# Two on-chip buffers that begin 32 bytes later in every partition

## The reference, cut to what matters

```python
x = x + lru_mlstm_layer(rmsnorm(x, e_norm[j]), ...)    # u = x @ w_in, ..., y @ w_out
x = x + ssd_layer(rmsnorm(x, o_norm[j]), ...)          # u = x @ w_in, ..., y @ w_out
hn = rmsnorm_2(h, norm_mix_w[l]);  proj = hn @ w_in[l]
h = h + merged.astype(h.dtype) @ w_out[l]
h = h + conv_gated_mlp(rmsnorm_2(h, norm_ffn_w[l]), ...)   # u = h @ w_up, ..., @ w_down
```

## The kernel before, in words

| buffer | first byte | remainder |
|---|---|---|
| RAW, WL | 16,512 | 0 |
| WH | 45,184 | 0 |
| XN | 65,664 | 0 |
| YS1, YS2, XMS, GOS, MS, HS | 114,720 | 32 |
| XCS, DOS, ZS | 131,104, 147,488, 176,160 | 32 |
| GE1, ST, KTM, YB | 143,392, 151,072, 146,464, 197,152 | 32 |
| HB | 216,768 | 0 |

## Time and profile before

### The profile page before, as it was taken

The page is one execution under the profiler, slowest core; times in us unless marked ns, Lnnn a source line. Parts: engine busy times, 40 slices in busy tenths (PEclk is TensorE's granted clock), DMA queues, the critical chain, the costliest instruction groups (busy, mean ns, idle before and its releaser), DMA issues.

```text
span 3152.4 us, 53605 instructions
## 1 busy us (share of the span) xinstructions
PE 3073.7 (98%) x21726; PEld 2844.2 (90%) x21726; DVE 2307.0 (73%) x3156; ACT 1841.7 (58%) x2374; POOL 540.2 (17%) x640
## 2 busy tenths in 40 slices
PE   7999999999999999999999999999999999999997
PEld 7989998889999999889888889999998888888886
DVE  7655888657788887676866887876666888887544
ACT  5554888645766776555664554445445666666443
POOL 1000000000000000145634555750001000000000
PEclk9999999999999999999999999999999999999999
DMA  5445445556555556665433445556555555555554
GB/s 209 155 149 178 156 156 180 178 189 212 185 185 182 180 182 208 196 202 195 154 124 124 148 140 170 173 173 210 185 187 187 189 192 188 192 188 191 190 188 139
DMA packets 158761, 560.50 MB, mean 178 GB/s; under 512 B 17760, under 2 KB 26016, under 8 KB 158000
## 3 DMA queue, kind: packets, MB, share of 16 engines
q1 hardware_dynamic: 158512, 557.06, 53.7%
HBM read 550.64 MB, written 6.36 MB: 177 GB/s over the span
## 4 chain that ended last, share of the span: by engine, by line
PE 85%; DVE 7%; ACT 5%; issue 2%; DMA 0%; POOL 0%; DVEq 0%; ACTq 0%; POOLq 0%; SPq 0%
PE ps L574 84%; DVE WL L1355 2%; ACT WH L921 2%; ACT L911 2%; DVE XC L1329 0%; DMA RAW<-in_w 0%; DVE XMC L1329 0%; DVE XC L1345 0%; ACT RS L911 0%; DVE IB L1318 0%; POOL RSB L1957 0%; DVE X L1329 0%; DVE HB L1318 0%; PE ps L750 0%; DVE BS L1318 0%
## 5 line engine op out<-in xcount | busy, mean ns | idle before, releaser
L574 PE MATMUL ps<-XN,WH 128*128 128x256 f32 (+1 forms) x8864 | 1855.4, 303 | 17.8 <-DVE WL L1355 11.7
L921 ACT ACTIVATE WH<-RAW 128x1024 fp32r<-128x1024 f32 x1010 | 1064.8, 1058 | 1110.2 <-PE ps L574 1058.8
L1355 DVE TENSOR_TENSOR WL<-RAW,WH 128x1024 fp32r<-128x1024 f32 x1010 | 1260.4, 1255 | 478.7 <-ACT WH L921 470.8
L574 PEld LDWEIGHTS ps<-XN,WH 128*128 128x128 f32 x8864 | 1435.4, 192 | 94.0 <-DVE WL L1355 12.7
L574 PE MATMUL ps<-XN,WL 128*128 128x256 f32 x5120 | 1445.4, 282 | 0.0
L574 PEld LDWEIGHTS ps<-XN,WL 128*128 128x128 f32 x5120 | 981.7, 192 | 0.0
L574 PE MATMUL ps<-YS,WH 128*128 128x512 f32 (+1 forms) x1088 | 371.4, 388 | 7.2 <-DVE YS L1318 3.8
L574 PE MATMUL ps<-YS,WL 128*128 128x256 f32 x1056 | 296.6, 281 | 0.0
L1957 POOL TENSOR_TENSOR RSB<-RSB,SQ 128x256 f32<-128x256 f32 x75 | 75.9, 1012 | 1220.8 <-ACT SQ L911 1218.6
L574 PEld LDWEIGHTS ps<-YS,WH 128*128 128x128 f32 x1088 | 203.6, 189 | 51.9 <-DVE WL L1355 4.2
L574 PE MATMUL ps<-HS,WH 128*128 128x512 f32 x688 | 238.6, 392 | 0.0
(11 more groups left out here) (332 smaller groups left out, 3325.2 us busy)
## 6 DMA issues: line engine op xcount, KB each, us to landing
RAW<-in_w SPq DMA_DIRECT2D x1010, 512.0 KB, 3.3
CSB<-sums SPq DMA_DIRECT2D x64, 128.0 KB, 3.8
X<-scratch SPq DMA_DIRECT2D x2, 2048.0 KB, 8.0
X<-in_x SPq DMA_DIRECT2D x1, 2048.0 KB, 8.0
scratch<-X SPq DMA_DIRECT2D x1, 2048.0 KB, 8.6
scratch<-X SPq DMA_DIRECT2D x4, 512.0 KB, 5.5
out<-X SPq DMA_DIRECT2D x4, 512.0 KB, 2.7
X<-in_x SPq DMA_DIRECT2D x3, 512.0 KB, 9.0
```

Source lines behind the costliest of these rows:

```text
L574: return pe.e.matmul(dst, l, r, start=start, stop=stop, skip_group_check=True)
L921: act.e.activation(WH[:, w % NH, :], RAW[:, w % NB, :], ACT.Copy).then_inc(*act.one(("wh", w)))
L1355: dve.e.tensor_tensor(WL[:, w % NB, :], RAW[:, w % NB, :], WH[:, w % NH, :].bitcast(F32), SUB).then_inc(*dve.one(("wl", w)))
```

## The change

Two lines are added to the placement. WH begins 32 bytes later, XN with it; a second step behind XN moves all that follows by 64 bytes.

```diff
         RAW = v3(fx("RAW", NB * UB * 128), NB)
         WL = v3(Map(nc, base, end)("WL", NB * UB * 128, F32R), NB)
+        fx.at += 32
         WH = v3(fx("WH", NH * UB * 128, F32R), NH)
         XN = v3(fx("XN", 16 * 512, F32R), 16)
+        fx.at += 32
         CV = fx("CV", NVEC)
```

## The result

The changed kernel took 3159.41 us in the median of 19 runs, the kernel before 3152.9 us in 19 runs beside it: a ratio of 1.0018 (95% interval 1.0012 to 1.0025), some 6 us slower. One of the changed kernel's 19 runs, in a slow state, took 4298.83 us and is left out of the ratio. The forecast was 3124 us. The time lies inside the stated range, but on the other side of the kernel before.

What follows compares the result with a forecast made beforehand. PE was taken to bound the kernel, its time the sum of its steps. XN's -27 us, all else nothing, gave 3152.4 - 27 = 3125.4 us of span, so 3124 us of time; whole range 3117 to 3168 us.

Steps and rivals of the forecast that it cites:

- What bounds the kernel: PE, busy 98% of the span; only its step lengths matter, and the weight pipeline waits for it.
- XN at 32: Form "f" over XN, 3,744 blocks from 0.360 to 0.352 us: 30.0 us, less a tenth, so -27 us.
- WH at 32 in form "w": One of two weight loads in form "w" comes from the moved WH; steps have slack, so nothing taken.
- The other inputs: ZS, XMS, DOS, GOS, XCS, YS in form "f", 736 blocks at remainder 32: cost 0 to 5.9 us, nothing taken.
- The rest: Form "t", 384 long matmuls, would be 1 us; a tenth off XN's gain for small matmuls and waits between blocks.
- Phase: Rival, 0.27: both places set form "f"'s pace; 3145 us, or 3157 if one slow step holds its two neighbours.
- Its other case: Under phase, over XN only WL's step of three gains, 9.7 us; the other inputs lose 3.8 us: 3145 us.
- Weights off the multiple of 64: Rival, 0.19: in form "f" each WH step costs 2.6 ns over the slow pace; +17 us, 3168 us.
- No effect: Rival, 0.08: form "f"'s pace follows something else differing between XN and ZS, such as higher address bits; 3151 us.
- the 16-byte lines: Rule against the forecast: 32 bytes are two whole SBUF lines, operands cover as many as before, time stays 3151 us.

Runs made afterwards that it cites:

- the second execution: The changed kernel profiled once more with nothing altered, to see whether its paces repeat; 3162.62 us, one run.
- the faster kernels above: Against the kernel before: XN by 32, others by 128, 0.9938; XN by 192, others by 256, 0.9918; XN by 192, MLP's inputs by 288, 0.9892.

## Why the prediction was wrong

**What bounds the kernel: right.** WL's 1257 ns and WH's 1060 ns stayed, and the waits for WL are 15.9 us instead of 15.1; what moved the time were PE's steps.

**XN at 32: the size near, the reason wrong.** The forecast took 27 us off form "f" over XN, and 27.0 us went; that they agree so closely is luck. The pace fell to 117.8 ns and not to ZS's 117.3, which gave 22.5 us, and the other 4.5 are less time at the lower clock, which the second execution didn't have. Above all, the step said that the streamed operand's own place sets the pace. XN at remainder 0 over WH at 0 and WL at 32 runs at 117.8 ns (RAW and WL moved), and XN at 0 over rings at 32 at 116.9 ns (all rings moved): it is the distance to the rings that counts. By the Trainium skill, page "SBUF — State Buffer", section "Who interferes with whom", the streamed operand and the weight load have independent read ports; no run here contradicts the ports as such, but the pace still depends on where the two operands lie relative to each other, 119.9 ns at (0, 0) and 114.9 at (192, 192). Why it does stays open.

**WH at 32 in form "w": the step that failed.** "In form 'w' a step has slack: XN and HS go at one pace with different remainders, so I take nothing there either." Two pairs with one pace, (0, 0) and (160, 160), were read as proof that no pair matters. The runs have form "w" at 0.347 us a block at (0, 0), (32, 32) and (160, 160), at 0.350 and 0.351 at (96, 96) and (128, 128), at 0.353 at (64, 64), (192, 192), (224, 224), (0, 32) and (32, 64), and at 0.347 or 0.351 at (192, 224). So form "w" had no slack that hides the places: in the changed kernel this term is +17.6 us, not 0, and it eats most of the gain in form "f".

**The other inputs: the same error.** They "keep remainder 32", but by 256 they went from (160, 160) to (192, 224). Form "f" lost 3.0 us, inside the stated 0 to 5.9; form "w" over YS, HS and MS lost 8.5 of the 17.6 us.

**The rest.** Steps among the small matmuls and form "t" took 9.5 us, where the forecast had 1 us and a tenth of its gain. Of form "t"'s 3.3 us some 2.7 are the lower clock (an estimate: half of the 5.5 us that it ran at 0.5; before it had none). The rest, mostly at the small matmuls, is in the faster kernels above too; its cause was not tested.

**The rivals.** "Phase" was right in kind, that the relation of the two places counts. That its 3157 us lie near the measured time is luck: in that case XN was to gain nothing, and form "w" was left out. Its other case had steps of 120 and 117 ns side by side, where the trace has 117.3, 118.3 and 117.8. "Weights off the multiple of 64" named the right side and is refuted: with WH and WL both off it the kernel is faster, 3142 us. "No effect" is refuted by the paces; with it what the prediction concluded from the 16-byte lines of the Trainium skill (page "SBUF — State Buffer", section "Door 1: The DMA port swizzle"), since shifts by whole lines moved the time from 0.9892 to 1.0034 of before.

## What to carry to other kernels

Where a matmul streams 256 or 512 columns and each has its own weight load, the distance between the streamed buffer and the weight buffer is worth trying as a tuning knob of its own; in this kernel it was worth 1%. A pad in front of one buffer moves all that follow, so pads are to be planned for every streamed buffer; here by 256 bytes rather than by 64. Two settings with the same time don't show that a knob is dead.

## What the runs showed of the hardware that was not expected

- Form "f" (three matmuls of 256 columns a block) had 119.9 ns a step at (0, 0), 116.9 at (32, 32), 114.9 at (192, 192); the pair that is best for it is among the worst for form "w".
- Moving both the weights and the input left XN's paces alone where the pair stayed: (32, 32) was reached with XN moved by 32 over rings in place, and by 64 over rings moved by 32, 116.9 ns and 0.347 us both times.
- Two patterns at one pair, 0.347 and 0.351 us a block over MS, in two executions of one program; and GOS and DOS at 119.9 or 117.8 ns a step with all that these matmuls read at the same bytes.
